# Norms by token tiles in a two-block transformer kernel, with the first four weight halves behind each norm taken tile by tile

## What is computed

```python
def first_block(x, ...):                      # depth 2
    for l in range(DEPTH):
        y = hybrid_mixer(x, w_in[l], ...)     # two attentions, a gated unit, pooling; y @ w_o
        x = layer_norm(DN_ALPHA * x + y, ln1_g[l], ln1_b[l])
        y = conv_gated_ffn(x, ...)            # 1024 -> 2*2816, conv, silu gate, 2816 -> 1024
        x = layer_norm(DN_ALPHA * x + y, ln2_g[l], ln2_b[l])

def second_block(x, mem, ...):                # depth 2
    for l in range(DEPTH):
        h = rmsnorm(x, norm_mix[l])
        ...                                   # DeltaNet, sparse attention, memory attention, gates
        x = x + merged @ w_out[l]
        h = rmsnorm(x, norm_ffn[l])
        gt, up = jnp.split(h @ w_ffn_in[l], 2, axis=-1)
        x = x + (jax.nn.silu(gt) * up) @ w_ffn_out[l]
    return rmsnorm(x, norm_final)
```

## Time and profile before

| | |
|---|---|
| median of 3 runs | 2334.2 us (2333.01 to 2335.53) |
| the profiled execution | 2335.5 us, its span 2333.4 us |
| PE busy | 94% of the span, 15336 instructions |
| POOL, ACT, DVE busy | 64%, 46%, 40% |
| mean granted TensorE clock | 0.961 |

### The profile page before, as it was taken

How to read it: one execution, slowest core, us unless ns; L and a number is a source line. 1 busy time by engine, 2 the same in 40 slices (tenths; PEclk the granted TensorE clock), 3 DMA queues, 4 the chain that set the end, 5 groups by cost and what they waited for, 6 DMA issues and landing times.

```text
span 2333.4 us, 35994 instructions
## 1 busy us (share of the span) xinstructions
PE 2182.3 (94%) x15336; PEld 2016.4 (86%) x15336; DVE 938.7 (40%) x1512; ACT 1072.1 (46%) x1511; POOL 1499.0 (64%) x632
## 2 busy tenths in 40 slices
PE   8999989899978989989999899899899899998997
PEld 7789977799868979879999899888789799998997
DVE  4342356422376546374112311456364561123113
ACT  4555555455545352345444444562522454544443
POOL 6688877698844233356778688662333566787885
PEclk9989999999979989999999999999989999999999
DMA  8345534355523122234445455342222344454553
GB/s 334 140 145 186 191 119 164 108 199 181 182 91 127 55 73 75 89 129 143 159 154 191 147 186 191 130 145 73 73 73 73 109 149 159 145 182 161 181 182 116
DMA packets 47183, 333.05 MB, mean 143 GB/s; under 512 B 5168, under 2 KB 5552, under 8 KB 7856
## 3 DMA queue, kind: packets, MB, share of 16 engines
q1 hardware_dynamic: 47024, 330.76, 41.0%
HBM read 329.69 MB, written 1.05 MB: 142 GB/s over the span
## 4 chain that ended last, share of the span: by engine, by line
PE 60%; DVE 8%; ACT 3%; issue 2%; POOL 0%; ACTq 0%; DVEq 0%
PE bank L146 14%; PE bank L148 13%; PE bank L147 13%; PE y L146 2%; PE y L148 2%; PE y L147 2%; PE bank L1679 2%; PE bank L1689 1%; DVE conv L1325 1%; PE bank L1612 1%; PE bank L1688 1%; DVE sc L2288 1%; PE bank L1734 1%; PE bank L1731 1%; PE bank L1507 1%
## 5 line engine op out<-in xcount | busy, mean ns | idle before, releaser
L336 POOL TENSOR_TENSOR w_lo<-w_raw,w_hi 128x1024 fp32r<-128x1024 f32 x602 | 1465.4, 2439 | 809.6 <-ACT w_hi L327 809.4
L327 ACT ACTIVATE w_hi<-w_raw 128x1024 fp32r<-128x1024 f32 x602 | 636.3, 1059 | 1055.5 <-PE bank L148 885.2
L146 PE MATMUL bank<-x_hi,w_hi 128*128 128x256 f32 x2960 | 881.0, 298 | 30.4 <-POOL w_lo L336 19.2
L147 PE MATMUL bank<-x_lo,w_hi 128*128 128x256 f32 x2960 | 851.8, 288 | 0.0
L148 PE MATMUL bank<-x_hi,w_lo 128*128 128x256 f32 x2960 | 851.6, 288 | 0.0
L146 PEld LDWEIGHTS bank<-x_hi,w_hi 128*128 128x128 f32 x2960 | 582.0, 197 | 57.1 <-issue 25.9
L147 PEld LDWEIGHTS bank<-x_lo,w_hi 128*128 128x128 f32 x2960 | 582.3, 197 | 10.6 <-issue 8.6
L148 PEld LDWEIGHTS bank<-x_hi,w_lo 128*128 128x128 f32 x2960 | 582.0, 197 | 0.0
L862 DVE SCALAR_TENSOR_TENSOR conv<-bank,par_sb,conv 128x254 f32<-128x254 f32 (+1 forms) x176 | 76.8, 478 | 255.0 <-ACT conv L850 253.5
L1188 DVE TENSOR_TENSOR hid_lo<-hid,hid_hi 128x512 fp32r<-128x512 f32 x22 | 44.8, 2038 | 246.7 <-ACT hid_hi L1183 246.7
L146 PE MATMUL y<-w_hi,hid_hi 128*128 128x512 f32 x352 | 139.2, 396 | 1.0 <-DVE hid_lo L884 1.0
(11 more groups left out here) (392 smaller groups left out, 3243.6 us busy)
## 6 DMA issues: line engine op xcount, KB each, us to landing
w_raw<-w SPq DMA_DIRECT2D x300, 1024.0 KB, 4.8
ln_rows<-ln_rows SPq DMA_DIRECT2D x4, 1024.0 KB, 5.8
mem_tok<-mem SPq DMA_DIRECT2D x2, 1024.0 KB, 7.0
const_sb<-const SPq DMA_DIRECT2D x1, 1536.0 KB, 9.1
par_sb<-par SPq DMA_DIRECT2D x2, 553.5 KB, 10.8
xn<-xT SPq DMA_DIRECT2D x1, 1024.0 KB, 4.9
w_raw<-w SPq DMA_DIRECT2D x2, 512.0 KB, 5.2
x_tok<-x SPq DMA_DIRECT2D x1, 1024.0 KB, 7.3
```

The source lines that it names most:

```text
L146: pe.matmul(out, lhs[0], rhs[0], start=start, stop=False, skip_group_check=skip)
L147: pe.matmul(out, lhs[0], rhs[1], start=False, stop=False, skip_group_check=skip)
L327: act.activation(self.hi[:, h % HALVES, :], self.raw[:, n % RAWS, i * HW:(i + 1) * HW], ACT.Copy).then_inc(*sig.up("high", h))
L336: pool.tensor_tensor(self.lo[:, h % HALVES, :], self.raw[:, n % RAWS, i * HW:(i + 1) * HW], self.hi[:, h % HALVES, :].bitcast(F32), ALU.su ...
```

## The change

It has these parts.

1. *Token order* (`by_tokens`). For the four halves that follow each norm except the last, PE takes token tile 0 of all four, then token tile 1 of all four. A half in layout features is then 48 matmuls of 128 columns in place of 24 of 256; in layout tokens the number stays. `product` of each of the four is signalled in the pass of tile 1. For the last norm, the four halves *before* it are ordered so. Features follow six of the norms (the next half pairs of `up0`/`val0`, `sm`/`q0`, `fin0`/`fval0`); behind `ln2` of layer 0 stand one half of features (`gate`) and three of tokens.
2. *Norms by tile.* All steps of tile 0 come before those of tile 1, except for one or two sums. ACT scales the second half of `xn`. In the RMS norms ACT sums the squares (`Square` with `accum_out`) instead of `bn_stats`. The table of the square root is loaded ahead (`preload_act_table_set`). PE turns tile 0, takes tile 0 of three halves, turns tile 1, and goes on.
3. *The double norm.* The last layer norm and the first RMS norm become one stage (`before=` in `Norm2`).
4. *Order of units.* The last down projections of each feed (8, 9, 10) come behind all up projections; banks 4 and 5 serve the first units behind a norm; some `high` instructions come later in ACT's program.
5. Semaphores of the two blocks are shared by name (`BOTH_BLOCKS`), and `y_hi` moves in SBUF.

```diff
@@ class Stream @@
+        self.parts = [(h, part) for h in range(len(self.halves)) for part in range(2)]
+        self.split = set()
+    def by_tokens(self, first):
+        group = range(first, first + HALVES)
+        self.split.update(group)
+        self.parts[2 * first:2 * (first + HALVES)] = [(h, part) for part in range(2) for h in group]
@@ def pe @@
-            h, part = p // 2, p % 2
+            h, part = self.parts[p]
...
-            if u.layout == "features":
+            if u.layout == "features" and h in self.split:
+                w = [v.rearrange("p (k c) -> p k c", k=KD) for v in (hi, lo)]
+                t = slice(part * P, (part + 1) * P)
+                for k in range(KD):
+                    if u.ready is not None and j == 0:
+                        u.ready(pe, k, part)
+                    mm = passes(pe, u.out[:, j * T + part * P:j * T + (part + 1) * P], [v[:, k, :] for v in w],
+                                [v[:, k, t] for v in u.x], k == 0, k == KD - 1)
...
@@ class Norm2, pe @@
         for tt in range(TT):
+            net.main.pe(pe, self.end() + tt * (HALVES - 1))
             for k in range(KD):
...
@@ class Norm2, act @@
+        main.act(act, self.end() - 6)
+        act.preload_act_table_set("sqrt_and_others")
+        root_before(0)
+        if self.before is not None:
+            main.act(act, self.end() - 2)
+        root(0)
+        main.act(act, self.end() - 4)
+        scaled(0)
+        main.act(act, self.end() - 2)
+        features(0)
+        main.act(act, self.end())
+        root_before(1)
+        root(1)
+        scaled(1)
+        features(1)
@@ class Norm2, dve @@
+        residual(0, 0)
+        residual(0, 1)
+        scaled(0)
+        residual(1, 0)
+        if self.key != "final":
+            for i in range(4):
+                split(0, i)
+        residual(1, 1)
+        scaled(1)
...
@@ class Net @@
+        for s in self.stages:
+            if isinstance(s, (Norm1, Norm2)):
+                last = s.after().last
+                if s.key == "final":
+                    self.main.by_tokens(last + 1 - HALVES)
+                if s.key != "final":
+                    self.main.by_tokens(last + 1)
```

More of the change, by code:

```diff
@@ L231, in handle @@
     def handle(self, name):
+        name = BOTH_BLOCKS.get(name, name)
         if name not in self.sems:
@@ L1020, in before @@
+        net.main.dve(dve, self.end())
+        for half in range(2):
+            statistics(0, half)
+        scaled(0)
+        statistics(1, 0)
+        for i in range(4):
+            split(0, i)
+        statistics(1, 1)
+        scaled(1)
+        for i in range(4):
+            split(1, i)
     def before(self):
@@ L1086, in act @@
     def act(self, act):
-        net, sig, k_l = self.net, self.net.sig, (self.key, self.l)
-        if self.after is not None:
-            net.main.act(act, self.end())
-        for tt in range(TT):
-            act.wait_ge(*sig.at("var", *k_l, tt))
-            act.activation(net.sd[:, tt:tt + 1], net.ms[:, tt:tt + 1], ACT.Sqrt).then_inc(*sig.up("root", *k_l, tt))
-        if self.key == "final":
-            return
-        if self.l == 0 and self.key == "norm_mix":
-            act.wait_ge(*sig.at("par2_loaded"))
@@ L1107, in dve, with added, residual @@
         step = net.dve_chain.step
-        if self.after is not None:
-            net.main.dve(dve, self.end())
-        for tt in range(TT):
+        def added(tt, half):
+            if tt == TT - 1 and half == 1:
+                dve.wait_ge(*sig.at("product", self.after().last))
+            else:
+                dve.wait_ge(*sig.at("summed", self.more, tt, half))
+            return net.y[:, tt * D + half * HALF:tt * D + (half + 1) * HALF]
+        def residual(tt, half):
+            c = slice(half * HALF, (half + 1) * HALF)
+            y = added(tt, half)
+            dve.tensor_tensor(net.xtok[:, tt, c], net.xtok[:, tt, c], y, ALU.add).then_inc(*sig.up("x_new", *k_l, tt, half))
@@ L1111, in dve, with normed_before @@
+        def normed_before(tt):
+            b = self.before
+            rows = net.ln_rows[b[0]]
             for half in range(2):
                 c = slice(half * HALF, (half + 1) * HALF)
[L1113 to L1119 removed]
@@ new lines, in dve @@
+        net.main.dve(dve, self.end())
+        if self.before is not None:
+            normed_before(0)
+            scaled(0)
+            for i in range(4):
+                split(0, i)
+            normed_before(1)
+            scaled(1)
+            for i in range(4):
+                split(1, i)
+            return
+        residual(0, 0)
+        residual(0, 1)
+        scaled(0)
+        residual(1, 0)
+        if self.key != "final":
+            for i in range(4):
+                split(0, i)
@@ L1151, in pool @@
+        residual(1, 1)
+        scaled(1)
+        if self.key != "final":
+            for i in range(4):
+                split(1, i)
     def pool(self, pool):
-        if self.after is not None:
-            self.net.main.pool(pool, self.end())
+        self.net.main.pool(pool, self.end())
     def sp(self, sp):
         net, sig = self.net, self.net.sig
+        if self.before is not None:
+            net.main.send(sp, net.main.halves[self.after().last][0] + 1 + 5)
         if self.key != "final":
```

317 lines of the change are left out of this document (177 added, 140 removed).

## The result

The changed kernel takes 2480.71 us (median of 4 runs, 2472.32 to 2481.83) against 2333.81 before (2333.01 to 2335.53): a ratio of 1.0621, 95% interval 1.0596 to 1.0645. That is 147 us slower. The forecast of 2352 us had the sign right and the size wrong by 129 us, outside its range.

The account below looks back on a forecast made before the run. The prediction took PE, busy 94% of the span, as the bound. Its terms, 19 + 13 - 1 - 7 - 6 = +18 us, made 2352 us on the median, with a range of 2317 to 2378.

Parts of the forecast that it names:

- s: Start-to-start spacing of 128-column float32r matmuls on PE, taken as 0.115 us; said to decide the case.
- (a): Rival: weight load does not bound PE, spacing 0.064 to 0.085 us, time 2318 to 2330 us; chance 0.18.
- (b): Rival: narrow float32r matmuls cost what plain ones do, 0.22 us each, +116 us, 2468 us; chance 0.12.
- rival (c): Clock stays at 1.2 GHz for tile 0's passes at five norms, +35 us, 2387 us; chance 0.09.
- the same loss: Slow-clock loss behind `ln1`, left at 1.3 us in a term of +6.5 us each, +13 for two.
- First matmul behind the RMS norms: Feature matmuls behind RMS norms would start 5.0 us after the last product of `y`, in place of 10.1.
- last norm: Token order at the kernel's end costs PE nothing and ends it near 2327.5 us, a gain of 6 us.
- the layer norms' first matmul: Behind `ln1`, the first matmul would come about 6.0 us after the last product, in place of 10.25.
- POOL's later start: POOL starts halves 5 to 8 only from PE's tile 1 pass; claimed to cost nothing new at s = 0.115.
- ln2: Behind layer 0's `ln2`, 4.2 us gained at the start and 2.8 lost in one feature half; taken as -1.
- the double norm: Fused last layer norm and first RMS norm: -2 us, -7 together with ACT being free sooner.
- The two `norm_ffn` terms: Behind `norm_ffn` of both layers, earlier start but 96 more matmuls: 28.0 us against 21.65, +6.3 each.

Follow-up runs that it names:

- filler: Changed kernel plus unused 256-column matmuls behind tile 0's transposes, 30 per layer norm and 12 per RMS norm: 2391.82 us, ratio 1.0243.
- POOL held: Changed kernel plus unused matmuls, with POOL's `low` instructions behind layer norms, except the first, held until tile 0's low part is made: 2373.22 us, ratio 1.0162.
- the narrow feed: Kernel before, with feature halves 31 to 90 of layer 0's feed taken by token tiles, 1920 passes of 128 columns: 2431.87 us.
- the last norm alone: Kernel before, with only the last four down halves and the last norm by token tiles: 2329.0 us, ratio 0.9972.

## Why the prediction was right or wrong

**s: the number right, its reason not shown.** I took 0.115; it is 0.111 to 0.112 at full clock, whether in the changed kernel, in the feed or behind filler. Rivals (a) and (b) are out. But I had worked it out from the weight load, 0.056 us for 64 more weight columns and so 0.11 for 128, and rows of the kernel before do not bear that out:

```profile
691.98 0.78 PE L1546 MATMUL bank<-const_sb,rowq 8*128 8x8 f32 x10
691.98 0.69 PEld L1546 LDWEIGHTS bank<-const_sb,rowq 8*128 8x128 f32 x10
```

Ten pairs of load and matmul with 128 weight columns (8 rows, 8 moving columns) are 0.062 us apart, so the prediction's sentence that no instruction with 128 weight columns comes as fast as 81 ns is wrong, and each of these loads lasts 0.136 us, as one of 128 rows and 64 columns does. The plain products that I called the nearest form say little about the load either: with 64 weight columns they are 0.109 apart (L1714), with 128 they are 0.111. No run keeps the weights and narrows the stream, so what holds the narrow float32r pass at 0.111 stays open, and that it came so near my number is in part luck. The Trainium skill's 81 ns for pairs of this width ("TensorE: Matmul & The Clock Gate", Back-to-back issue gap) was not seen with float32r weights.

**The clock: the step that failed.** The prediction put it as rival (c), "the clock stays at its 1.2 GHz level for the passes of tile 0", +35 us and a chance of 0.09, with "against it: full-rate streams recovered within 5 us". Those were wide streams, and I applied their recovery to narrow ones. My own sum put the clock at nothing new ("I leave the same loss in, 1.3 us"). What the runs showed: narrow passes do not bring the clock back (58 us without a gap at half), and behind the RMS norms they do not even hold it. So not 72 but up to all 192 passes per norm ran at 0.213, and at seven norms, not five: 105 us where (c) had 35. That narrow passes stay at the low clock was right in (c); its size was three times too small, its chance far too low. Whether it is for the reason that (c) gives, an array half filled while loads bound it, no run shows. The range's upper end, 2378, also left out (c)'s own 2387.

**The norms' start and the end: right.** First matmul behind the RMS norms at 4.8 us (5.0 said), tail 6.5 (6.5 said), last norm -5.9 (-6 said).

**POOL beside DVE: missing.** I wrote that the layer norms' first matmul would come after about 6.0 us and that POOL's later start "costs nothing new". It came at 8.3, and `x_lo` of the following k as late as 14 us after the last product. Three `low` instructions run during the norm now (117.09 to 124.83), where the kernel before had one (115.91), and a cast, a subtraction or a scaling on DVE that meets one can take some 2.5 us. The trace of the kernel before had it already, at the same norm, beside POOL's write of `x_tok`:

```profile
119.68 1.43 POOL L1035 TENSOR_TENSOR x_tok<-xn,ln_rows 128x512 f32<-128x512 f32 x1 [1.42 <-DVE xn L997]
120.09 2.71 DVE L997 TENSOR_SCALAR xn<-x_tok,mv,rs 128x512 f32<-128x512 f32 x2
```

The same two scalings of the other tile took 1.00 us there. I had named "copies are split on DVE" and POOL's load in one section without laying one beside the other. It is worth 19 us between the two runs with filler, 12 of them by way of the clock.

**ln2 and the double norm: mis-sized.** Even at nearly full clock their stretches are +8.1 and +10.6, not -1 and -7. At the double norm DVE's `x_tok` pair (L1229) takes 5.35 us beside POOL's `w_lo`, so first transposes come at 10.6 us, where the prediction had 6 in one place and a whole chain of about 8 in another. Of its +10.6, 4.2 are there by the eighth half behind the norm, and 6.4 come in the mixer behind it. For `ln2` I left out tile 0's delayed split altogether. The two `norm_ffn` terms, 6.3 each, are 5.4; that of `norm_mix` is 5.7 by the eighth half, and the mixer behind it gives 4.1 back. The prediction named a shift of the mixers by more than 2 us as a sign of being wrong; it came, and its cause was not looked for. With the clock nearly full, what I called the sum (+18) is +38.

**The order of sizes.** 147 is, within 1 us, 101 for the clock (89 with filler, 12 more with POOL held), 7 for the waits on DVE beside POOL, and 38 for passes of double number less the earlier starts, with the double norm's stretched pair in it. The first is shown by filler, by the passes of 256 columns in the same order and by the count of slow passes (105 us), and the time that POOL's hold takes back by that run; how its 19 us part into 12 and 7 is worked out from the count of passes, and the third is what is left.

## What to carry to other kernels

Before narrowing a stream behind a wait, look at the granted clock there. In these traces a clock lowered at a wait was paid again in nearly every narrow pass that followed, mostly until something wide ran; idle PE time can be filled with unused wide matmuls, and that gained even where nothing was narrowed (2329.0 to 2320.6 us). And when work is moved on one engine, lay the DVE and POOL timelines of the new overlap beside each other: an operation's time from the old trace holds only for its old neighbours.

## What the hardware showed that was not expected

- The clock depends on what came before. The same narrow passes ran at 0.111 us where they began at full clock in a stream without waits (1920 of them in one feed) and at 0.213 for up to 92 us where they began at half. Behind a wait of 1.4 and one of 1.5 us they began at full clock and lost it after 1.5 us (1369.70 to 1371.2); passes of 256 columns behind the same waits kept it. It came back behind passes of 256 columns within 5 us of them (1410.9 to 1415.6) or behind ones of 512 (4.8 us). Three times it rose within 3 us of the start of plain fp32 transposes that interrupted narrow passes (733.41 to 736.4 in the changed kernel, 138.56 to 140.5 and 486.67 to 488.7 with filler); behind the same transposes at 1383.70, and at four more norms of the changed kernel, it did not. What tells those cases apart stays open.
- How long the clock is down behind a wait differs between executions of the same instructions: behind `ln1` of layer 0 it was down for 10.2 us in the kernel before and for 3.4 us in two runs whose program is the same up to there (119.8 to 123.2, the narrow feed and the last norm alone).
- At half clock a pass of 256 columns is spaced 0.213 too, so there the narrow pass costs what the wide one does.
- A cast of 0.28 us on DVE took 2.44 beside a POOL subtraction of 2.4 us, and fell back to 0.29 when POOL was held; statistics of 0.69 us were not stretched.
